# A two-layer mixer block and its follow-up on one core: input projection on raw input, weight splits on VectorE, feed-forward parts made tile by tile

## Chip, cores and metric

The kernel runs on one core of a Trainium2 chip. The metric is the device time of one execution in microseconds (us); smaller is better. Before the change three runs took 2217.0, 2222.6 and 2223.59 us, median 2222.6.

## The reference, cut to what matters

512 tokens of width 1024 pass two layers (`DEPTH = 2`), and then a second, different block that the change doesn't touch. One layer is:

```python
h = rmsnorm(x, attn_norm[l])
z = h @ w_in[l]                                    # 1024 -> 2256 columns
(c_q, c_kv, k_rope, g_q, g_k, g_v, g_lr, g_g, r_q, r_k, r_v, r_g) = jnp.split(z, ...)
y_a = mla_branch(...)     # q = rmsnorm(c_q) @ w_uq, k and v = rmsnorm(c_kv) @ w_ukv, causal softmax, 4 heads
y_b = gla_branch(...)     # gated linear attention, 4 heads, its gate from g_lr
y_c = retention_branch(...)                        # 4 heads, rope on q and k
x = x + jnp.concatenate([y_a, y_b, y_c], -1) @ w_out[l]
h = rmsnorm(x, ffn_norm[l])
u = h @ ffn_w_up[l]                                # 1024 -> 2 * 2816
a, bv = u[..., :D_FF], u[..., D_FF:]
x = x + (silu(causal_dwconv(a)) * bv) @ ffn_w_down[l]
```

`rmsnorm` multiplies by a gain for each feature and by one factor for each token (the inverse root of the mean square). The factor is the same for all features of a token, so it may be applied after the product with the weights: that is what the kernel calls raw.

## The kernel before, in words

**Layout.** `x_t` holds x turned: features on the 128 partitions, 8 tiles of 512 tokens. Every product with a weight is made three times in the float32r format: activations and weights are each split into a high part (a rounded copy, `h_hi`, `w_hi`) and a low part (value minus high part, `h_lo`, `w_lo`), and high x high, high x low and low x high are summed. Lines L823 to L825 issue them in `product`.

**Weights** come in chunks of up to 1024 x 256 (1 MB) into two slots of `w_raw`, alternately. Chunk c goes through: a DMA on SyncE's queue (`load`, issued when the low half of chunk c-2 has been made), `w_hi` copied by ScalarE (`high`, `next_high`, when TensorE is done with chunk c-2), `w_lo` subtracted by GpSimd (L1010, in the first part of a layer) or by VectorE (`split_low`, L1835, in the feed-forward), and two tiles of products on TensorE, each 128 output features x 512 tokens, or 2 x 128 tokens x 256 columns for those whose output is wanted with tokens on the partitions. A counter `w_split` releases TensorE. All of it is written out by hand, each engine with its own list of instructions in order, and semaphores between them.

**Order of a layer** (chunks and tiles by number: chunk c has tiles 2c and 2c+1):
- Chunk 0 is multiplied with raw parts of x (made at the end of the layer before, without the token factor), `raw_tiles`. Meanwhile the token factor `rms_a` is formed, and VectorE and ScalarE form normed parts h_hi and h_lo (`parts_dve`, L812 and L797; `parts_act`, L786) in place, one of the 8 feature tiles after the other. Chunk 1 (`two_tiles`, L847 to L849) follows these step by step, with the small matmul of the linear attention's gate (`gate_low`, L1122) in its middle.
- Chunks 2 to 8 (tiles 4 to 17) use the normed parts. ScalarE copies each finished tile out of PSUM (L1418). Between the tiles stand the matmuls of the linear attention: for seven decay levels VectorE forms two products (L1939, L1941) and a difference (L1880), ScalarE an exponential, TensorE 32 small matmuls (`pairs`, L1087), and VectorE keeps a part of their results with a predicated copy (`keep`, L1890). Turn, state update and output of this branch follow (L1094, L1101, L1111, L1114).
- Chunks 9 to 15 are the up-projections of q, k and v, with contraction over 3 and 2 tiles only, and in between the matmuls that swap halves for the rope (L1165 to L1168). VectorE applies the rope (`rope`, L1823 to L1827). Its table comes by a DMA ahead of the load of chunk 15, after all of q's tiles.
- The attention goes over 16 instances (`att_pe`, `att_act`, `att_dve`): scores (L466), mask and maximum (L557, L562), exponential (L521), turn (L475), copy (L515), values (L486), and after every fourth the normalisation (L543, L547). The retention branch runs in its gaps, as functions in `fill` by instance number: rope halves, pairs, weights, turn, update, output.
- The out-projection (chunks 16 to 19) needs y turned, a tile at a time (`turn_y`, L1210), and its parts (`high_y` L1563, `low_y` L1994). Two tiles are turned in the attention, six in the first chunk. Before these, `lin_gated` (L1931) must be done for the retention, and GpSimd scales `y_mla` by the factor of each head (L1026).
- ScalarE copies each output tile, VectorE adds it to x_t (L2016), squares and sums it (L1789, L1791). After the last tile the statistic is formed (L763), and then parts of x for the feed-forward (L1592, L1994), again raw.
- Up loop: 22 chunks of 11 pairs; down loop: 12 chunks. Then the next layer.

## Time and profile before

| | |
|---|---|
| median of 3 runs | 2222.6 us |
| the profiled execution's own time | 2222.46 us |
| its span | 2220.5 us |
| mean granted TensorE clock | 0.967 |
| TensorE busy | 2054.5 us, 93% |
| VectorE busy | 1121.5 us, 51% |
| ScalarE busy | 855.1 us, 39% |
| GpSimd busy | 435.7 us, 20% |

Both layers run the same loop body. Layer 0's ends at about 700 us, layer 1's at about 1358 us, and the second block takes the rest. Busy TensorE isn't TensorE at full speed: matmuls overlap, and their length grows when the granted clock is at its lower level (0.50, 1.2 GHz) and not the upper one (1.00, 2.4 GHz).

### The profile page before, as it was taken

How to read it: one execution, taken by the hardware profiler on the slowest of the kernel's cores; microseconds unless marked ns; L12 is line 12 of the kernel's file. 1: busy time of each engine (PE TensorE's matmuls, PEld its weight loads, DVE VectorE, ACT ScalarE, POOL GpSimd, SP SyncE). 2: the span in 40 equal slices, each digit the busy share in tenths (PEclk: the TensorE clock that was granted, in tenths of full speed). 3: DMA queues.
4: the chain of work that ended last, by engine and by line, in shares of the span. 5: the costliest groups of instructions: out<-in, count | busy, mean ns of one | idle time of the engine just before them, and what ended most of it. 6: DMA issues, size and time to landing. Idle time of an engine off the chain costs nothing.

```text
span 2220.5 us, 28741 instructions
## 1 busy us (share of the span) xinstructions
PE 2054.5 (93%) x10802; PEld 1647.7 (74%) x10802; DVE 1121.5 (51%) x1222; ACT 855.1 (39%) x1212; POOL 435.7 (20%) x178
## 2 busy tenths in 40 slices
PE   5998889999999998889999998899999899899987
PEld 3786578888886886678888886887777566788765
DVE  6754665555536755665555446515552522313353
ACT  4444443333213444333333223234445455534333
POOL 3323030000000313030000001432222222343441
PEclk9998989999999999999999999999999899999998
DMA  5213023333232213023333223323322112132230
GB/s 139 76 41 114 1 70 82 94 94 94 85 104 74 76 42 114 1 76 92 97 95 94 85 90 119 115 67 102 80 85 66 52 48 77 57 105 84 69 104 38
DMA packets 236697, 177.72 MB, mean 80 GB/s; under 512 B 11700, under 2 KB 231215, under 8 KB 236207
## 3 DMA queue, kind: packets, MB, share of 16 engines
q1 hardware_dynamic: 235664, 174.74, 26.3%
q8 instruction: 69, 1.13, 0.2%
q10 hardware_dynamic: 575, 1.50, 0.2%
q0 software_dynamic: 352, 0.05, 0.1%
q14 instruction: 37, 0.30, 0.0%
HBM read 167.87 MB, written 2.10 MB: 77 GB/s over the span
## 4 chain that ended last, share of the span: by engine, by line
PE 68%; DVE 11%; issue 10%; POOL 5%; ACT 4%; DMA 2%; SPq 1%; ACTq 0%; DVEq 0%; POOLq 0%
PE ps L823 19%; PE ps L825 19%; PE ps L824 18%; POOL w_lo L1010 4%; PE ps L466 2%; PE ps L591 2%; PE ps L604 1%; PE ps L615 1%; POOL w_lo L1036 1%; ACT w_hi L1654 1%; PE ps L486 1%; PE ps L475 1%; DVE h_lo L2197 1%; DVE qk L2092 1%; DMA gains_in<-in_ffn_conv_w_dram 0%
## 5 line engine op out<-in xcount | busy, mean ns | idle before, releaser
L823 PE MATMUL ps<-h_hi,w_hi 128*128 128x512 f32 x1488 | 599.1, 403 | 17.6 <-ACT qk L1418 6.2
L825 PE MATMUL ps<-h_hi,w_lo 128*128 128x512 f32 x1488 | 587.1, 395 | 0.0
L824 PE MATMUL ps<-h_lo,w_hi 128*128 128x512 f32 x1488 | 582.9, 392 | 0.0
L1036 POOL TENSOR_TENSOR w_lo<-w_raw,w_hi 128x1024 fp32r<-128x1024 f32 (+1 forms) x118 | 264.9, 2268 | 930.2 <-ACT w_hi L1654 930.2
L823 PEld LDWEIGHTS ps<-h_hi,w_hi 128*128 128x128 f32 x1488 | 282.6, 190 | 83.7 <-DVE h_lo L1994 9.0
L825 PEld LDWEIGHTS ps<-h_hi,w_lo 128*128 128x128 f32 x1488 | 281.6, 189 | 65.1
L824 PEld LDWEIGHTS ps<-h_lo,w_hi 128*128 128x128 f32 x1488 | 282.3, 190 | 60.6 <-issue 1.0
L1010 POOL TENSOR_TENSOR w_lo<-w_raw,w_hi 128x2048 fp32r<-128x2048 f32 (+2 forms) x42 | 154.3, 3676 | 702.3 <-ACT w_hi L1425 684.7
L1425 ACT ACTIVATE w_hi<-w_raw 128x2048 fp32r<-128x2048 f32 (+3 forms) x108 | 186.7, 1729 | 203.1 <-PE ps L825 196.2
L1835 DVE TENSOR_TENSOR w_lo<-w_raw,w_hi 128x2048 fp32r<-128x2048 f32 (+1 forms) x68 | 151.6, 2230 | 195.3 <-ACT w_hi L1425 193.2
L823 PE MATMUL ps<-w_hi,h_hi 128*128 128x256 f32 x480 | 139.0, 290 | 6.9 <-POOL w_lo L1036 6.4
L823 PE MATMUL ps<-hid_hi,w_hi 128*128 128x512 f32 x352 | 138.7, 394 | 0.0
L825 PE MATMUL ps<-hid_hi,w_lo 128*128 128x512 f32 x352 | 138.0, 392 | 0.0
L824 PE MATMUL ps<-hid_lo,w_hi 128*128 128x512 f32 x352 | 136.6, 388 | 0.0
L824 PE MATMUL ps<-w_lo,h_hi 128*128 128x256 f32 x480 | 136.0, 283 | 0.0
L825 PE MATMUL ps<-w_hi,h_lo 128*128 128x256 f32 x480 | 135.7, 283 | 0.0
L1654 ACT ACTIVATE w_hi<-w_raw 128x1024 fp32r<-128x1024 f32 (+1 forms) x118 | 108.2, 964 | 13.9 <-DMA w_raw<-in_w_in_dram 12.1
L1603 ACT ACTIVATE rms_a<-a_pad,g 128x512 f32<-128x512 f32 x44 | 35.9, 816 | 173.5 <-DVE a_pad L2031 173.5
L823 PEld LDWEIGHTS ps<-w_hi,h_hi 128*128 128x128 f32 x480 | 92.4, 193 | 9.4 <-POOL w_lo L1036 6.6
L2036 DVE SCALAR_TENSOR_TENSOR rms_a<-a_pad,g,rms_a 128x512 f32<-128x512 f32 x88 | 66.2, 752 | 57.1 <-ACT rms_a L1603 50.5
L699 DVE TENSOR_TENSOR ps<-ps,win 128x768 f32<-128x768 f32 x32 | 30.9, 966 | 124.9 <-PE ps L591 124.4
L824 PEld LDWEIGHTS ps<-w_lo,h_hi 128*128 128x128 f32 x480 | 92.8, 193 | 0.7 <-issue 0.5
(367 smaller groups left out, 3009.0 us busy)
## 6 DMA issues: line engine op xcount, KB each, us to landing
w_raw<-in_ffn_w_up_dram SPq DMA_DIRECT2D x88, 512.0 KB, 4.8
w_raw<-in_w_in_dram SPq DMA_DIRECT2D x41, 1024.0 KB, 5.1
w_raw<-in_w_in_dram SPq DMA_DIRECT2D x32, 512.0 KB, 4.9
w_raw<-in_ffn_w_down_dram SPq DMA_DIRECT2D x32, 512.0 KB, 4.3
w_raw<-in_w_out_dram SPq DMA_DIRECT2D x12, 1024.0 KB, 4.8
w_raw<-in_ffn_w_down_dram SPq DMA_DIRECT2D x16, 384.0 KB, 3.3
swapped<-qk SPq DMA_DIRECT2D x96, 64.0 KB, 2.0
w_raw<-in_w_mem_kv_dram SPq DMA_DIRECT2D x4, 1024.0 KB, 4.8
```

Of the source, the lines that this page charges most:

```text
L466: ins = pe.matmul(score_ps(banks, i, c0, n), lhs, rhs, start=a, stop=b)
L591: ins = pe.matmul(ps[:, b, c:c + n], lhs, rhs, start=True, stop=True)
L823: pe.matmul(dst, lh, rh, start=first and j == 0, stop=False)
L824: pe.matmul(dst, lh, rl, start=False, stop=False)
L825: ins = pe.matmul(dst, ll, rh, start=False, stop=last and j == len(order) - 1)
L1010: pool.tensor_tensor(w_lo[:, slot, 0:n], w_raw[:, slot, 0:n], w_hi[:, slot, 0:n].bitcast(F32), ALU.subtract).then_inc(sem("w_split"), 1)
L1036: ins = pool.tensor_tensor(w_lo[:, slot, q * n:q * n + n], w_raw[:, slot, q * n:q * n + n], w_hi[:, slot, q * n:q * n + n].bitcast(F32), A ...
L1425: act.activation(w_hi[:, slot, 0:n], w_raw[:, slot, 0:n], ACT.Copy).then_inc(sem("w_high"), 1)
L1603: act.activation(conv[:], a_pad[:, s, 2:S + 2], ACT.Identity, scale=g[:, bass.ds(G_CONVW + 2 * KF + f, 1)], bias=g[:, bass.ds(G_CONVB + f, ...
L1654: act.activation(w_hi[:, slot, q * n:q * n + n], w_raw[:, slot, q * n:q * n + n], ACT.Copy).then_inc(sem("w_high"), 1)
L1835: dve.tensor_tensor(w_lo[:, slot, 0:n], w_raw[:, slot, 0:n], w_hi[:, slot, 0:n].bitcast(F32), ALU.subtract).then_inc(sem("w_split"), 1)
L2036: dve.scalar_tensor_tensor(conv[:], a_pad[:, s, w:w + S], g[:, bass.ds(G_CONVW + w * KF + f, 1)], conv[:], ALU.mult, ALU.add).then_inc(sem ...
```

## The change

It does the following in both layers:
- The whole input projection (chunks 0 to 8) uses the raw parts. No normed parts are formed. VectorE takes the feature tiles out of PSUM itself (`evict`) and multiplies by `rms_a`; for token tiles ScalarE applies the factor as a scale for each partition, in two half copies (`copy_tokens`), after TensorE has turned `rms_a` into columns (`tok_rms`).
- All low halves of the layers' weights after the first two are made by VectorE (`split`), at written places of its list; GpSimd does nothing in the layers after those two.
- The decay levels start one tile earlier. The chunk of the retention's gate comes before the one of its values, and the rope part of w_uq before the two others. The rope's table is loaded after chunk 4. The retention's swap matmuls and ropes come ahead of the attention and not in it.
- The out-projection's parts have buffers of their own (`y_hi`, `y_lo`), its tiles the banks 0, 2, 1, 3. `y_mla` is scaled by VectorE in four parts within the attention and behind it. Four tiles of y are turned in the attention, four in the first chunk of the out-projection.
- VectorE adds each output tile to x_t right from PSUM, and the feed-forward's parts of this tile follow at once, in `h_hi` and `h_lo`. The first up tile stands before the statistic, and the up loop is rotated by one tile.
- Tanh for both gates is done in one place; two changes of ScalarE's function table go in each layer.

```diff
@@ SyncE
-                    if c == C_OUT - 1:
-                        sp.wait_ge(sem("tile_done"), upto(sp, "tile_done", 2 * C_UKV))
+                    if c == 4:
                         sp.dma_start(tab[:], A["c_rope"]).then_inc(sem("tab_loaded"), tick("tab_loaded", 16))
@@ GpSimd
-            with pool.Fori(0, DEPTH) as l:
...
-                    split(c, c % 2, SPLIT_K[c])
...
-                        pool.tensor_tensor(ym, ym, stats[:, 96:112].unsqueeze(2).to_broadcast([P, 16, VDIM]),
-                                           ALU.mult).then_inc(sem("ymla"), tick("ymla"))
@@ TensorE
-                        two_tiles(pe, 1, KD, h_hi, h_lo, (2, 3), (P, P), PART["x"], before={4: (0,)}, turn=gate_low)
-                    elif t > 3:
+                        features(pe, 1, 0, KD, h_hi, h_lo, 2, last=False, order=range(4))
+                        gate_low()
+                        features(pe, 1, 0, KD, h_hi, h_lo, 2, first=False, order=range(4, KD)).then_inc(sem("tile_done"), tick("tile_done"))
+                    elif t > 2:
                         tile(t, KD, h_hi, h_lo, kind)
...
-                    if 6 <= t < 6 + len(LEVELS):
+                    if 5 <= t < 5 + len(LEVELS):
...
+                    if t == 2 * C_UKV + 1:
+                        pe.wait_ge(sem("roped"), upto(pe, "roped", 1))
+                        for j in range(2):
+                            pe.matmul(ps[:, 4 + 3 * j, :], swap32, lin[:, 2 + j, :], start=True, stop=True).then_inc(sem("rot"), tick("rot"))
...
+                att_pe(pe, mla_groups(), prob, prob_t, fill={
+                    0: partial(ret_pairs, 0), 2: partial(ret_pairs, 2), 4: ret_turn, 6: ret_update, 8: partial(ret_out, 0),
+                    9: partial(ret_out, 1), 12: partial(turn_y, 0), 13: partial(turn_y, 1), 14: partial(turn_y, 2),
+                    15: partial(turn_y, 3)})
...
+                two_tiles(pe, C_OUT % 2, KD, y_hi, y_lo, OUT_BANKS[0:2], (P, P), PART["y"], Y_ORDER,
+                          before={3: (4, 5), 4: (6,), 5: (7,)}, turn=turn_y)
...
+                up_tile(0, 0, 0)
                 sum_stat(pe, 8)
-                with pe.Fori(0, KF // 2) as i:
+                with pe.Fori(0, KF // 2 - 1) as i:
+                    up_tile(i, 0, 1)
+                    up_tile(i, 1, 0)
+                    up_tile(i, 1, 1)
+                    up_tile(i + 1, 0, 0)
@@ VectorE
-                parts_dve(dve, 0, normed(dve, xs, col(G_ATTN, 8), rms_a[:], 0), hi, lo, fulls1, after={3: raw_scaled})
+                diff(0)
+                evict(2, lin[:, 0], LIN_DK ** -0.5)
+                evict(3, lin[:, 1])
+                level(0)
+                split(3)
+                evict(4, cq[:, 0])
+                keep(0, len(LEVELS))
...
+                for i in range(len(LEVELS)):
+                    if i < 3:
+                        evict(5 + i, cq[:, 1 + i])
+                    keep(i + 1, i)
+                    if i + 1 < len(LEVELS):
+                        level(i + 1)
+                    if i % 2 == 0:
+                        split(4 + i // 2)
+                evict(12, lin[:, 2])
...
+                split(14)
+                rope(3, lin[:, 2], ps[:, 4, :], tab[:, 2], tab[:, 3], lin[:, 2], tmp[:, 2])
+                split(15)
+                rope(4, lin[:, 3], ps[:, 7, :], tab[:, 2], tab[:, 3], lin[:, 3], tmp[:, 2])
...
+                    0: partial(ret_weights, 0), 1: ret_decayed, 2: partial(ret_weights, 2), 3: partial(split, 16),
+                    4: partial(mla_squares, 0), 5: partial(split, 17), 6: partial(lin_update, 1, um_r, (3, 7), lambda t: ret_c),
+                    7: partial(mla_scaled, 0), 8: partial(mla_squares, 1), 10: partial(lin_squares, 1, o_sb_r, um_r),
+                    11: partial(mla_scaled, 1), 12: lambda: (mla_squares(2), lin_gated(1, o_sb_r, sig_r, LIN["ret"]["gate"])),
+                    13: partial(low_y, 0), 14: lambda: (mla_squares(3), low_y(1))})
+                mla_scaled(2)
+                low_y(2)
+                low_y(3)
+                mla_scaled(3)
...
+                    dve.tensor_tensor(x_t[:, m], x_t[:, m], ps[:, OUT_BANKS[m], :], ALU.add).then_inc(sem("tile_copied"), 1)
...
+                    if m % 2:
+                        split(C_OUT + 2 + m // 2)
```

## Rows read from the trace of the kernel before

**Rows 1.** The page, the chain that ended last: shares of the span by engine.
```profile
PE 68%; DVE 11%; issue 10%; POOL 5%; ACT 4%; DMA 2%; SPq 1%; ACTq 0%; DVEq 0%; POOLq 0%
```

**Rows 2.** Busy time by windows, layer 1; columns as in the first line.
```profile
core 0: us, PE busy (x) PEld busy (x) DVE busy (x) ACT busy (x) POOL busy (x), PEclk, DMA share, GB/s
706.60:726.40 19.80, 14.87 (x51) 9.99 (x51) 17.66 (x19) 6.54 (x9) 4.68 (x1) 0.91 0.17 55
726.40:835.90 109.50, 103.53 (x845) 91.48 (x844) 63.92 (x56) 46.30 (x62) 30.05 (x7) 0.95 0.17 50
835.90:870.20 34.30, 28.30 (x137) 21.65 (x135) 16.09 (x15) 20.06 (x30) 15.18 (x8) 1.00 0.38 123
870.20:925.40 55.20, 52.37 (x278) 34.36 (x278) 35.20 (x65) 22.59 (x57) 4.21 (x1) 0.94 0.12 39
925.40:980.20 54.80, 49.50 (x217) 40.29 (x216) 32.79 (x32) 15.50 (x21) 17.92 (x4) 0.94 0.18 50
980.20:988.20 8.00, 2.23 (x4) 0.52 (x3) 6.57 (x4) 7.49 (x10) 4.52 (x1) 0.68 0.22 55
988.20:1358.70 370.50, 370.50 (x1608) 303.86 (x1609) 200.11 (x216) 116.79 (x114) 0.00 (x0) 0.99 0.32 94
```

**Rows 3.** The same view, three windows of layer 0.
```profile
66.50:173.30 106.80, 100.28 (x844) 88.84 (x843) 64.55 (x56) 46.14 (x61) 30.02 (x7) 0.98 0.17 52
173.30:212.30 39.00, 28.32 (x136) 21.64 (x135) 20.36 (x15) 20.44 (x30) 19.12 (x8) 0.91 0.41 135
267.90:321.80 53.90, 48.66 (x216) 39.68 (x216) 32.79 (x32) 15.40 (x21) 17.92 (x4) 0.97 0.18 50
```

**Rows 4.** TensorE's waits, 700 to 1000 us: total us, times, longest us.
```profile
PE ps L1087 <- DVE gl L1941: 6.0, 3, 2.2
PE ps L847 <- DVE h_lo L797: 4.9, 3, 3.0
PE ps L466 <- DVE qr L1827: 4.8, 1, 4.8
PE ps L1210 <- DVE tm L1931: 4.1, 1, 4.1
PE ps L823 <- DVE h_lo L1994: 2.9, 1, 2.9
...
PE ps L475 <- ACT prob_t L515: 2.0, 2, 1.4
```

**Rows 5.** Busy time by windows again, three short stretches of layer 1.
```profile
720.80:723.60 2.80, 2.71 (x6) 2.15 (x7) 2.35 (x5) 0.63 (x1) 0.00 (x0) 0.50 0.71 224
760.30:768.70 8.40, 8.34 (x83) 7.99 (x84) 5.22 (x7) 3.12 (x5) 0.00 (x0) 0.80 0.39 126
768.60:775.30 6.70, 6.70 (x82) 6.50 (x80) 5.34 (x3) 2.51 (x2) 3.81 (x1) 1.00 0.00 0
```

**Rows 6.** Timeline of all engines, 754.4 to 760.4 us: start, length, instruction.
```profile
754.43 4.60 POOL L1010 TENSOR_TENSOR w_lo<-w_raw,w_hi 128x2048 fp32r<-128x2048 f32 x1 [8.20 <-ACT w_hi L1425]
...
754.94 4.64 DVE L1939 TENSOR_TENSOR gl<-lin,gl 128x512 f32<-128x512 f32 x1
```

**Rows 7.** The page, costliest groups: count, busy us, mean ns, idle before.
```profile
L1425 ACT ACTIVATE w_hi<-w_raw 128x2048 fp32r<-128x2048 f32 (+3 forms) x108 | 186.7, 1729 | 203.1 <-PE ps L825 196.2
L1835 DVE TENSOR_TENSOR w_lo<-w_raw,w_hi 128x2048 fp32r<-128x2048 f32 (+1 forms) x68 | 151.6, 2230 | 195.3 <-ACT w_hi L1425 193.2
```

**Rows 8.** VectorE's groups by shape, 726 to 836 us, columns as above.
```profile
L1890 DVE COPY_PREDICATED amat<-levels,ps 128x2048 f32<-128x2048 uint8 x8 | 19.9, 2488 | 17.3 <-issue 15.5 <-DVE gl L1880 1.8
L1939 DVE TENSOR_TENSOR gl<-lin,gl 128x512 f32<-128x512 f32 x7 | 17.1, 2446 | 0.2
L1880 DVE TENSOR_TENSOR gl<-gl 128x512 f32<-128x512 f32 x7 | 4.8, 692 | 0.2
```

**Rows 9.** TensorE's timeline, one row of the attention, one behind it.
```profile
874.50 3.29 PE L1174 MATMUL ps<-lin,cm 128*128 128x512 f32 x4
...
940.81 0.60 PE L1210 MATMUL ps<-cm,y_mla 128*128 128x128 f32 x4
```

More of the change, by code:

```diff
@@ L1155, in _ @@
                 for t in range(2 * C_UQ, 2 * C_UKV):
[L1156 to L1166 removed]
+                    tile(t, 3, cq_hi[:, 0:3], cq_lo[:, 0:3])
@@ L1169, in _ @@
                 pe.wait_ge(sem("tile_copied"), upto(pe, "tile_copied", 2 * C_OUT))
-                pe.wait_ge(sem("roped"), upto(pe, "roped", 3))
-                def ret_halves():
-                    for j in range(2):
-                        pe.matmul(ps[:, 3 * j, :], swap32, lin[:, 2 + j, :], start=True, stop=True).then_inc(sem("rot"), tick("rot"))
+                pe.wait_ge(sem("roped"), upto(pe, "roped", 5))
                 def ret_pairs(first):
-                    if first == 0:
-                        pe.wait_ge(sem("roped"), upto(pe, "roped", 5))
-                    else:
+                    if first:
@@ new lines, in up_tile @@
+                def up_tile(i, s, half):
+                    c = C_UP + 2 * i + s
+                    if half == 0:
+                        split_ready(c)
+                    pe.wait_ge(sem("tile_copied"), upto(pe, "tile_copied", 2 * c + half - 3))
+                    features(pe, s, half, KD, h_hi, h_lo, 2 * s + half,
+                             ready=PART["ffn"] if s + half == 0 else None).then_inc(sem("tile_done"), 1)
+                up_tile(0, 0, 0)
+                sum_stat(pe, 8)
@@ L1933, in lin_gated, with level @@
                     dve.wait_ge(sem("y_lin"), upto(dve, "y_lin"))
-                diff(0)
-                keep(0, len(LEVELS))
-                for i in range(len(LEVELS)):
+                def level(i):
                     dve.wait_ge(sem("lvl_exp"), upto(dve, "lvl_exp", i + 1))
```

358 lines of the change are left out of this document (191 added, 167 removed).

## The prediction

> **What bounds the kernel now.** I read the page first: the chain that ended last is 68% TensorE and 11% VectorE [rows 1], so time is set by TensorE's queue wherever something else is late. Next came the windows by stage, layer 1 and layer 0 [rows 2, 3]. The reader is to see two kinds of stretch. In the feed-forward loops (988.2 to 1358.7) TensorE is busy for 370.5 of 370.5 us with 1608 matmuls, 0.230 us each: nothing can be won there. In the other windows of layer 1 the busy time falls short: 4.9 us in the second weight chunk, 6.0 in the rest of the input projection, 6.0 in the up-projections of the attention, 2.8 in the attention, 5.3 in the out-projection and 5.8 before the feed-forward loop. That is 31 us in one layer, and the clock column is below 1.00 in most of these windows, so part of the busy time is stretched as well. The change works on just these windows; up loop, down loop and second block keep their instructions (one up tile moves, one chain starts earlier).
>
> Third, the waits [rows 4]. All that matter name VectorE: 6.0 us in 3 waits for the decay levels (L1941), 4.8 us for the last rope (L1827), 4.1 us for the gated retention output (L1931), 4.9 us in 3 waits for the low parts of h (L797), 2.9 us for those of the feed-forward (L1994). Fourth, why VectorE is late [rows 6]: GpSimd splits a weight chunk from 754.43 for 4.60 us; VectorE's product of two SBUF tiles, issued at 754.94, takes 4.64 us and ends when GpSimd does. The group of that line has 7 instructions with a mean of 2446 ns, against 692 ns for the same shape in the next group [rows 8]. VectorE is held for the whole of GpSimd's instruction.
>
> The Trainium skill, "SBUF — State Buffer", section "Who interferes with whom", says the same: a VectorE instruction with two SBUF inputs contends with a GpSimd instruction that reads SBUF, and whoever issues first keeps the shared ports for its whole instruction. By that rule all two-input VectorE work beside a split is exposed, and with GpSimd silent none is; the trace agrees, with 4.64 against 0.69 us [rows 6, 8].
>
> Fifth, the price of a wait beyond itself [rows 5]: after the 2.2 us wait, pairs and a token tile took 8.4 us at a mean clock of 0.80; the same work without a wait in front took 6.7 us at 1.00. So each such wait costs another 1.7 us at the lower level. Six matmuls behind the 3.0 us wait for L797 [rows 4] took 2.8 us at 0.50, against 6 x 0.230 = 1.4: 1.4 us lost.
>
> **Change part by part**, layer 1 unless said.
>
> A. Chunk 1 no longer waits for normed parts. Now: 19.8 us [rows 2]. After: the raw h parts of chunk 0 are used again, and chunk 1's low half has long been made. 48 x 0.230 = 11.0, the gate matmul 1.0 (an estimate: 4 to 5 plain matmuls), four one-column turns 0.4: 12.4. Gain 7.4. The gate waits for VectorE's two evictions (2 x 0.7 us behind the raw tiles), while TensorE has 12 matmuls, 2.8 us, in front of it: covered. The 16 instructions of the normed parts (8 products, 8 subtractions) leave VectorE and 8 copies leave ScalarE; 10 evictions, of 0.69 us like other 512-wide products [rows 8], come to VectorE instead, token tiles get two half copies on ScalarE. I take the same gain in layer 0.
>
> B. Chunks 2 to 8. Now 109.5 us in layer 1, 106.8 in layer 0. The 3 waits (6.0) and their lower clock (3 x 1.7) go, leaving 98.4 in either: gains 11.1 and 8.4. That holds only if VectorE keeps up. Per pair of tiles it has two times (predicated copy 2.49 + q 0.69 + k 0.69 + difference 0.69 + eviction 0.69) = 10.5 and one split of 2.3 (mean 2230 ns over two sizes, most of them the larger [rows 7]): 12.8, with some 0.04 between instructions 13.3. TensorE takes 2 x 6.7 = 13.4. Equal, so the order decides. After the pairs of a tile end, the copy, q and k take 4.0 us, and TensorE wants them 5.6 us later; difference, split and eviction (3.8) lie behind, pushing the next copy by about 1.1 us. Slack at the worst place is near 0.5 us. The token tiles (four of eight) have no eviction on VectorE. I take no wait. The weight side: next high half is copied once the slot's last tile is done, about 1.9 us (mean 1729 ns over four sizes [rows 7]), then 2.3 us of split, while 13.4 us of the other slot run: covered. Waiting behind split(8) there are the evictions and q and kv parts, some 8 us, against 27 us until it is needed.
>
> C. Up-projections. Now 34.3 us (39.0 in layer 0), of which 6.0 us is unbusy; in layer 0, 10.7. The table loads with chunk 4 and not at the end, and the ropes meet no GpSimd split. Content 28.3; the two swap matmuls of the retention come in, 1.9 us (an estimate: half of the 3.3 us they have now at the lower clock, rounded up [rows 9]); at the end one ScalarE copy behind a 1.9 us high half, 1.3. Together 31.5: gains 2.8 and 7.5. These chunks are short, 2.8 us for two tiles of the smallest, and a tile copy of some 0.7, a high half and a split of a quarter of the width, some 0.6 each by the share of rows 7, and the gaps make 2.2, with a rope of 2.2 in VectorE's queue in front. The split of chunk 15 comes only 0.8 us ahead. Without that cover each of four chunks would pay up to 2.2.
>
> D. Attention. Now 55.2. The swap matmuls go (-3.3 [rows 9]), the waits for prob_t too (-2.0 [rows 4]), and after 1.3 us of idle instead of 4.8 the first scores run faster: the clock of 0.94 means 12% of the window at half speed, 3.3 us lost; I take back 1.5. In come two turns of y at most 0.6 each [rows 9] (+1.2), and VectorE's fills. Two splits (4.6), two scalings, two gatings (2.5) now sit between the maxima; three ropes and a silu go. Following the queue, the fifth value product waits for the first normalisation (+1.4), the last score for squares, gating and third normalisation (+1.7). Gain 2.5. Bounds: all of it hidden, 5.6; each split fully on the path, -2.1.
>
> E. Out-projection. Now 54.8 and 53.9 us. Contents 192 x 0.230 = 44.2, four turns left 2.4. After the last value product VectorE does normalisation 1.0, squares 1.4, low part 0.8 before the second k step may start, 3.3 us, while TensorE has 1.4: wait 1.9, then 0.2 for the turns; the low clock again, 1.4. Sum 50.1: gains 4.7 and 3.8. GpSimd's 4 us scaling of y_mla becomes four small VectorE ones of 0.7.
>
> F. Feed-forward start. Now 8.0, and six matmuls at half speed behind it (1.4). After: the parts of x follow tile by tile. VectorE needs per tile addition, square, low part and sum, 4 x 0.73 = 2.9, and per two tiles a split 2.3: 8.1 of the 11.0 us that TensorE needs. The last part is ready 3.5 us after the last tile (high half 1.9 on ScalarE first, copy, low part); the first up tile wants it after 7 steps, 4.8 us. Only the statistic remains, 0.5. Gain 8.9. rms_f then comes some 2 us behind the first up tile; four banks hide this.
>
> Sum, layer 1: 7.4 + 11.1 + 2.8 + 2.5 + 4.7 + 8.9 = 37.4; layer 0: 7.4 + 8.4 + 7.5 + 2.5 + 3.8 + 8.9 = 38.5. Together 75.9; for short waits where I found slack below 1 us (B, C) I give back 1 per layer. 2220.5 - 73.9 = 2146.6 for the span. The profiled execution took 2222.46, 2.0 more than its span, and the median of the runs is 2222.6. Forecast 2148.6, said as 2148.
>
> **Rivals.**
> 1. VectorE becomes the bound in B. For: 13.3 against 13.4. Against: only three of eight tiles carry an eviction. If four levels are 0.6 late, each with 1.7 of lower clock: 9 us a layer, 2166. Chance 0.15.
> 2. The fills stall the softmax. For: a split is one instruction of 2.3 us that a maximum can't pass. Each split and the gating on the path: 2 x 2.3 + 2.5 = 7 a layer, 2162. Chance 0.12.
> 3. The waits of E and D don't appear, since the chains overlap better than I follow them: -(1.9 + 1.4 + 1.4 + 1.7) a layer, 2135. Chance 0.13.
> 4. Slower. Weight loads are issued only after the low half of the chunk two before; that now stands in VectorE's queue. The 36 splits of both layers would each have to be late by 76/36 = 2.1 us beyond their slack to eat the gain, 2.3 for a loss over 0.3%: 2231. Against: in the up loop, VectorE already makes its splits, and TensorE is busy throughout [rows 2]. Chance 0.02.
> 5. The change doesn't do what it says: TensorE merely waits elsewhere, for ScalarE, within 0.3%: 2220. ScalarE is busy 46.3 of 109.5 us [rows 2], so I give 0.01.
> The forecast has 0.57.
>
> **Numbers.** 0.3% (some 7 us) is about what this measurement can tell from no change. Range 2134 to 2168: it takes in rivals 1 to 3 and the bounds of D, and leaves out some 1 in 10. Faster 0.97, same 0.01, slower 0.02.
>
> **What the profile after would show.** GpSimd silent between the first two splits and the second block; L1939's product at 0.69; no wait of the level pairs; stages near 12.4, 98, 31, 53, 50 and 0.5 us; the feed-forward loops at 370. Wrong: level pairs waiting for the predicated copy (rival 1), first value products waiting for normalisation by more than 2 us (rival 2), or TensorE waiting for w_lo from VectorE anywhere (rival 4).

## The result, and the profile after

| | before | after |
|---|---|---|
| median of the runs | 2219.8 us (4 runs, 2209.2 to 2223.6) | 2161.4 us (4 runs, 2154.1 to 2167.2) |
| ratio, 95% interval | | 0.9743, 0.9691 to 0.9794 |
| profiled execution, its span | 2222.46, 2220.5 us | 2166.44, 2164.7 us |
| VectorE, GpSimd busy | 1121.5, 435.7 us | 1105.0, 283.8 us |

The kernel is 2.6% faster. The forecast was 2148, the range 2134 to 2168. The span fell by 55.8 us (26.7 in layer 1, 27.0 up to its start, 2.1 in the second block) where the prediction's sum had 73.9.

Busy time by windows of the changed kernel, layer 1; the stages are those of [rows 2], and the feed-forward's start is now its first up tile, 936.10 to 942.00:

```profile
core 0: us, PE busy (x) PEld busy (x) DVE busy (x) ACT busy (x) POOL busy (x), PEclk, DMA share, GB/s
679.60:693.10 13.50, 13.50 (x62) 10.61 (x61) 9.23 (x10) 7.21 (x10) 0.00 (x0) 1.00 0.46 159
693.10:792.20 99.10, 99.10 (x846) 87.60 (x844) 71.41 (x72) 42.09 (x58) 0.00 (x0) 1.00 0.19 56
792.20:823.00 30.80, 28.92 (x139) 22.34 (x138) 14.61 (x21) 15.24 (x23) 0.00 (x0) 1.00 0.32 103
823.00:887.50 64.50, 61.97 (x281) 42.02 (x282) 37.52 (x63) 25.16 (x64) 0.00 (x0) 0.76 0.10 33
887.50:936.10 48.60, 46.60 (x212) 37.60 (x211) 34.58 (x43) 13.86 (x17) 0.00 (x0) 1.00 0.22 60
936.10:942.00 5.90, 5.90 (x27) 4.67 (x26) 4.24 (x5) 2.53 (x2) 0.00 (x0) 1.00 0.16 42
942.00:1305.00 363.00, 363.00 (x1587) 297.64 (x1586) 195.76 (x210) 116.16 (x113) 0.00 (x0) 1.00 0.33 96
```

The same view, layer 0: the up-projections and the attention.

```profile
160.70:191.70 31.00, 28.95 (x140) 22.37 (x139) 14.61 (x21) 15.24 (x23) 0.00 (x0) 1.00 0.33 102
191.70:256.10 64.40, 61.89 (x282) 41.94 (x283) 37.51 (x63) 25.18 (x64) 0.00 (x0) 0.76 0.10 33
```

The reader is to see one row that doesn't fit. Every other stage of layer 1 runs at a clock of 1.00 and takes what was forecast to within 1.5 us. The attention became longer, 64.5 us against 55.2 in [rows 2], though less stands still in it: TensorE is busy for 62.0 us of it, and its clock is 0.76 where it was 0.94.

TensorE's waits in the changed kernel, 680 to 942 us (total us, times, longest us):

```profile
PE ps L848 <- DVE y_lo L2051: 2.0, 1, 2.0
PE ps L476 <- ACT prob_t L516: 1.9, 1, 1.9
PE ps L467 <- ACT v_mla L1428: 1.9, 1, 1.9
PE ps L1201 <- DVE tm L1959: 0.6, 1, 0.6
```

All waits of [rows 4] for the level pairs, the low parts of h, the rope and the feed-forward's parts are gone. The 11.8 us that the attention is above the forecast (64.5 against 52.7) are not in waits: TensorE stands still for 2.5 us of it. Windows again, inside the attention of layer 1:

```profile
825.00:831.00 6.00, 6.00 (x30) 4.47 (x28) 3.42 (x9) 2.52 (x11) 0.00 (x0) 0.51 0.00 0
...
843.00:849.00 6.00, 6.00 (x15) 2.99 (x15) 5.00 (x7) 1.63 (x6) 0.00 (x0) 0.50 0.43 146
849.00:853.00 4.00, 4.00 (x15) 3.46 (x14) 0.65 (x2) 1.56 (x5) 0.00 (x0) 0.57 0.79 262
853.00:859.00 6.00, 6.00 (x32) 3.78 (x31) 4.80 (x10) 1.55 (x4) 0.00 (x0) 1.00 0.01 1
```

TensorE is busy 6.00 of 6.00 us at its lower level (0.50, 1.2 GHz) for some 27 us on end, in both layers. In the kernel before, the attention started at the lower level too:

```profile
212.30:222.00 9.70, 9.68 (x23) 5.84 (x24) 4.70 (x11) 1.65 (x7) 0.00 (x0) 0.50 0.33 108
870.20:877.30 7.10, 7.10 (x17) 4.28 (x18) 2.58 (x8) 2.00 (x8) 4.21 (x1) 0.52 0.68 222
877.30:884.40 7.10, 6.63 (x41) 4.18 (x41) 6.37 (x12) 1.44 (x6) 0.00 (x0) 1.00 0.22 73
```

There the clock rose 9.7 us (layer 0) and 7.1 us (layer 1) into it: 1.4 us behind the two retention swaps of 512 columns in layer 0, in the last half microsecond of them in layer 1 [rows 9]. The change had moved just these two out of the attention, into the up-projections, where they run at the upper level. TensorE's groups by shape, 792 to 823 us (the trace has two records for each of the two matmuls):

```profile
L1165 PE MATMUL ps<-lin,cm 128*128 128x512 f32 x4 | 1.9, 592 | 0.0
```

That gives a theory (the clock theory: without the swaps the attention's first part is only short matmuls, and the clock stays low through them) and a rival: VectorE's new fills, two weight splits above all, hold the softmax up, and the clock merely follows.

### The profile page after: what moved, and what is told of

Read it like the earlier page. It is cut to its first block, busy times and chain, and to the rows that moved or that the text cites. A ratio compares the mean times of both kernels' runs of the same rounds, so it can differ in the third digit from the quotient of the medians.

```text
span 2164.7 us, 28562 instructions
## 1 busy us (share of the span) xinstructions
PE 2050.3 (95%) x10818; PEld 1649.5 (76%) x10818; DVE 1105.0 (51%) x1254; ACT 827.6 (38%) x1186; POOL 283.8 (13%) x136
## 4 chain that ended last, share of the span: by engine, by line
PE 84%; DVE 7%; ACT 4%; DMA 2%; POOL 1%; issue 1%; SPq 0%; ACTq 0%; DVEq 0%
PE ps L824 23%; PE ps L826 22%; PE ps L825 22%; PE ps L467 3%; PE ps L592 2%; PE ps L605 1%; PE ps L616 1%; POOL w_lo L1024 1%; PE ps L487 1%; PE ps L1075 1%; ACT w_hi L1667 1%; PE ps L476 1%; PE ps L1102 1%; DMA w_raw<-in_w_out_dram 1%; PE ps L757 1%
## 5 line engine op out<-in xcount | busy, mean ns | idle before, releaser
L824 PE MATMUL ps<-h_hi,w_hi 128*128 128x512 f32 x1408 | 565.8, 402 | 11.8 <-ACT qk L1428 6.2
L826 PE MATMUL ps<-h_hi,w_lo 128*128 128x512 f32 x1408 | 553.5, 393 | 0.0
L825 PE MATMUL ps<-h_lo,w_hi 128*128 128x512 f32 x1408 | 549.8, 390 | 0.0
L1848 DVE TENSOR_TENSOR w_lo<-w_raw,w_hi 128x2048 fp32r<-128x2048 f32 (+3 forms) x108 | 222.6, 2061 | 234.7 <-ACT w_hi L1435 229.1
L824 PEld LDWEIGHTS ps<-h_hi,w_hi 128*128 128x128 f32 x1408 | 266.0, 189 | 73.3 <-issue 9.6
L826 PEld LDWEIGHTS ps<-h_hi,w_lo 128*128 128x128 f32 x1408 | 265.0, 188 | 61.1
L825 PEld LDWEIGHTS ps<-h_lo,w_hi 128*128 128x128 f32 x1408 | 265.8, 189 | 57.0 <-issue 1.4
L824 PE MATMUL ps<-w_hi,h_hi 128*128 128x256 f32 x448 | 127.1, 284 | 4.4 <-POOL w_lo L1024 4.4
L825 PE MATMUL ps<-w_lo,h_hi 128*128 128x256 f32 x448 | 125.5, 280 | 0.0
L826 PEld LDWEIGHTS ps<-w_hi,h_lo 128*128 128x128 f32 x448 | 85.5, 191 | 0.0
```

Of the source, the lines that this page charges most:

```text
L824: pe.matmul(dst, lh, rh, start=first and j == 0, stop=False)
L825: pe.matmul(dst, lh, rl, start=False, stop=False)
L826: ins = pe.matmul(dst, ll, rh, start=False, stop=last and j == len(order) - 1)
L1848: dve.tensor_tensor(w_lo[:, slot, 0:n], w_raw[:, slot, 0:n], w_hi[:, slot, 0:n].bitcast(F32), ALU.subtract).then_inc(sem("w_split"), 1)
```

## The experiments

All are edits of the changed kernel. Attention is the time from the first score matmul to the out-projection's first product in the profiled execution, layer 0 and layer 1, with the mean clock. Spans and stages are those of one execution each; the medians are of four to six.

| kernel | median us | ratio to before, 95% | span | attention, clock |
|---|---|---|---|---|
| changed | 2161.4 | 0.9743 (0.9691 to 0.9794) | 2164.7 | 64.4 at 0.76, 64.5 at 0.76 |
| e1_burst | 2149.2 | 0.9669 (0.9646 to 0.9692) | 2147.9 | 56.8 at 0.94, 55.4 at 0.97 |
| e2_fill | 2142.1 | 0.9638 (0.9615 to 0.9661) | 2140.3 | 58.7 at 0.85, 53.6 at 0.97 |
| e3_both | 2140.4 | 0.9643 (0.9619 to 0.9666) | 2138.3 | 53.8 at 1.00, 55.0 at 0.98 |
| e4_pool | 2180.5 | 0.9826 (0.9797 to 0.9855) | 2175.2 | 59.9 at 0.83, 59.8 at 0.83 |
| e5_stat_first | 2168.6 | 0.9761 (0.9735 to 0.9786) | 2160.6 | 62.9 at 0.78, 58.4 at 0.85 |
| e6_low_first | 2144.0 | 0.9655 (0.9632 to 0.9679) | 2137.7 | 57.0 at 0.94, 53.8 at 1.00 |
| e7_pool_two | 2137.9 | 0.9630 (0.9602 to 0.9657) | 2136.1 | 54.0 at 0.97, 54.0 at 0.97 |
| e8_one_each | 2149.7 | 0.9680 (0.9644 to 0.9715) | 2144.6 | 60.9 at 0.83, 53.3 at 1.00 |
| e9_parts_late | 2172.4 | 0.9782 (0.9748 to 0.9815) | 2173.8 | 62.8 at 0.78, 64.4 at 0.76 |
| e10_swaps_back | 2150.7 | 0.9692 (0.9660 to 0.9724) | 2144.0 | 59.7 at 0.94, 59.8 at 0.91 |
| e11_both_more | 2140.5 | 0.9652 (0.9621 to 0.9683) | 2136.9 | 54.4 at 0.97, 53.5 at 1.00 |
| e12_back_fill | 2148.8 | 0.9682 (0.9650 to 0.9714) | 2150.8 | 61.3 at 0.86, 58.9 at 0.97 |

A span is a rough measure of an edit: the second block, which no edit touches, differs by itself. Here is everything behind layer 1 in the changed kernel and in e10_swaps_back, 9.0 us apart; in e1_burst it took 859.9 us, in e2_fill, e7_pool_two and e8_one_each 853.4.

```profile
1305.00:2164.70 859.70, 785.55 (x4427) 625.96 (x4425) 342.16 (x369) 364.74 (x588) 265.80 (x118) 0.96 0.26 79
```

```profile
1293.30:2144.00 850.70, 783.80 (x4432) 625.37 (x4431) 341.67 (x370) 365.50 (x589) 266.02 (x118) 0.97 0.26 79
```

The firmer measure is the length of the stage that an edit touches.

### Long matmuls at the attention's start

e1_burst adds work behind the first scores, e2_fill in the wait ahead of them, e3_both at both places.

```diff
+                pe.wait_ge(sem("roped"), upto(pe, "roped", 3))               # e2, e3
+                for _ in range(2):
+                    pe.matmul(ps[:, 5, :], swap64, qr[:, 0, :], start=True, stop=True)
                 pe.wait_ge(sem("tile_copied"), upto(pe, "tile_copied", 2 * C_OUT))
...
+                def burst():                                                 # e1, e3
+                    for _ in range(2):
+                        pe.matmul(ps[:, 7, :], swap32, lin[:, 2, :], start=True, stop=True)
...
-                    0: partial(ret_pairs, 0), 2: partial(ret_pairs, 2), 4: ret_turn,
+                    0: lambda: (burst(), ret_pairs(0)), 2: partial(ret_pairs, 2), 4: ret_turn,
```

> The changed kernel, with two 512-column fp32 matmuls added on TensorE in each layer, behind the first score group of the attention, ahead of the retention pairs; their result is not used. They stand where the kernel before had its two retention swaps. Clock theory: the 12 us that each layer's attention took above the forecast are TensorE's low granted clock (0.50 for some 27 us), and it is low for long because the retention swaps, behind which the clock rose in the kernel before, are no longer in the attention. Then the clock rises some 10 us into the attention, the attention takes 55 to 58 us in place of 64.5 (the added work of about 3 us included), and the span falls from 2164.7 to between 2147 and 2155. Rival: the two weight splits that VectorE now makes inside the attention (and the other added fills) hold the softmax up, and the clock is only a consequence of TensorE's waits; then the attention keeps its 64.5 us plus up to 3.3 us of added work, and the span is 2165 to 2172.

> The changed kernel, with two 512-column fp32 matmuls added in each layer just before TensorE waits for the last copy of the up-projections (the 1.9 us wait ahead of the first scores); their result is not used. Clock theory, first form: the fall to 0.50 at the start of the attention is set off by that idle time; filled, the clock stays at 1.00 and the attention takes about 53 us in place of 64.5, span about 2142. Clock theory, second form: what sets the clock off is the attention's own thin start (many short matmuls with their loads), and the idle time before it only hastens it; then less than 2 us per layer change, span 2161 to 2168. Rival (VectorE's fills hold the softmax up): no change, span 2164 to 2168.

> Both additions: two unused 512-column matmuls ahead of the attention's first wait, and two behind its first score group, in each layer. Clock theory: the attention takes 53 to 57 us, at or below the shorter of the two kernels with one addition each; span 2142 to 2152. If the first addition alone keeps the clock up, this one is slower than it by the 1.7 us per layer of the second pair at full clock. Rival (VectorE's fills): 64.5 us plus the added work, span 2168 to 2172.

The attention by windows, layer 0 and layer 1: first e1_burst, then e2_fill, then e3_both.

```profile
191.56:248.38 56.82, 53.18 (x287) 35.54 (x287) 37.32 (x63) 25.27 (x64) 0.00 (x0) 0.94 0.12 38
815.22:870.60 55.38, 51.52 (x286) 34.85 (x287) 37.34 (x63) 25.20 (x64) 0.00 (x0) 0.97 0.11 39
```

```profile
190.16:248.86 58.70, 55.99 (x282) 37.68 (x283) 37.41 (x63) 25.24 (x64) 0.00 (x0) 0.85 0.11 37
815.87:869.43 53.56, 49.91 (x283) 34.36 (x283) 37.32 (x63) 25.25 (x64) 0.00 (x0) 0.97 0.13 40
```

```profile
189.70:243.47 53.77, 50.12 (x286) 33.34 (x287) 37.32 (x63) 25.25 (x64) 0.00 (x0) 1.00 0.12 40
811.37:866.36 54.99, 51.27 (x286) 34.59 (x287) 37.33 (x63) 25.25 (x64) 0.00 (x0) 0.98 0.12 39
```

More work made the kernel faster, by 12 to 21 us at the median. The cleanest pair is layer 1 of the changed kernel and of e2_fill: inside the attention they have the same instructions (282 or 283 records of TensorE, 63 of VectorE, 64 of ScalarE) and take 64.5 us at 0.76 and 53.6 us at 0.97. VectorE's busy time is 37.5 and 37.3. So 10.9 us are the clock's, and the rival, which had no change or a loss in all three, falls. Two results differ from what was expected: e3_both's span of 2138.3 lies below its range, and e2_fill did in layer 1 what the first form of the theory said and in layer 0 half of it.

The form of the theory that blames the wait alone falls too. In e2_fill the wait ahead of the scores is down to 0.24 us in layer 0, and the clock still fell 3 us later, for some 17 us; in e1_burst it was 1.00 from the first score of layer 1 on, behind a wait of 1.8 us, and fell only at the attention's end (0.63 from 866.00 to 870.60). What the added matmuls change is how often and how long it is low, not by a fixed amount.

The Trainium skill, "TensorE: Matmul & The Clock Gate", section "What's actually happening", has the lower clock as the default and activity as what releases it, and its section "HAM oscillation — how this bites in real kernels" blames waits for the fall. That more work brings the clock up agrees with e1_burst (0.94 and 0.97 in place of 0.76). That an engine without idle time stays at 0.50 for 27 us is not what the page lets one expect: here it was 6.00 busy of 6.00 us.

### The step itself undone

e10_swaps_back adds no work: the two swaps go back behind the first score group, VectorE's retention rotation with them, and the retention's later steps follow two groups later. e12_back_fill is the same with the matmuls of e2_fill.

```diff
-                    if t == 2 * C_UKV + 1:
-                        pe.wait_ge(sem("roped"), upto(pe, "roped", 1))
-                        for j in range(2):
-                            pe.matmul(ps[:, 4 + 3 * j, :], swap32, lin[:, 2 + j, :], start=True, stop=True).then_inc(sem("rot"), tick("rot"))
...
-                    0: partial(ret_pairs, 0), 2: partial(ret_pairs, 2), 4: ret_turn, 6: ret_update, 8: partial(ret_out, 0),
-                    9: partial(ret_out, 1), 12: partial(turn_y, 0), 13: partial(turn_y, 1), 14: partial(turn_y, 2),
+                    0: ret_halves, 2: partial(ret_pairs, 0), 4: partial(ret_pairs, 2), 6: ret_turn, 8: ret_update,
+                    10: partial(ret_out, 0), 11: partial(ret_out, 1), 12: partial(turn_y, 0), 13: partial(turn_y, 1), 14: partial(turn_y, 2),
...
-                rope(3, lin[:, 2], ps[:, 4, :], tab[:, 2], tab[:, 3], lin[:, 2], tmp[:, 2])
...
+                    0: ret_rope, 1: ret_decayed, 2: partial(ret_weights, 0), 3: partial(split, 16),
```

> The changed kernel with one step undone and no work added: the two retention swap matmuls (512 columns each) are moved back from the fourth up-projection tile into the attention, behind its first score group, and VectorE makes the retention rotation there, as in the kernel before; the retention's later steps follow two groups later. Clock theory: it is this move that left TensorE at the low granted clock; with the swaps back in the attention the clock rises some 5 to 10 us into it, the attention takes 55 to 60 us in place of 64.5 (about 1.5 us of swaps and 1 us of short waits included), the up-projection stage loses 1 us, and the span is 2146 to 2158. Rival (only added work keeps the clock up, the place of the swaps is without effect, or the later retention steps hold up the last groups): attention 63 us or more, span 2162 or more.

> The same kernel with the swaps back in the attention, and with the two unused 512-column matmuls in the wait ahead of the first scores, as in e2_fill. Clock theory: full clock from the start in most layers, attention 53 to 56 us, span 2135 to 2145, as with the two additions of e3_both but with one useful pair in the place of one unused. Rival: the late retention steps cost more than the clock gives back: 2145 to 2160.

Windows of e10_swaps_back: around the swaps in layer 0, the same in layer 1, and a third place of layer 1.

```profile
189.54:196.54 7.00, 7.00 (x17) 4.21 (x18) 2.46 (x7) 3.45 (x8) 0.00 (x0) 0.53 0.00 1
196.54:202.54 6.00, 5.65 (x36) 3.47 (x34) 5.49 (x10) 1.01 (x4) 0.00 (x0) 0.98 0.00 0
816.06:822.06 6.00, 6.00 (x18) 3.46 (x19) 2.57 (x8) 3.45 (x8) 0.00 (x0) 0.72 0.00 0
822.06:828.06 6.00, 5.28 (x36) 3.40 (x35) 5.52 (x10) 1.01 (x4) 0.00 (x0) 1.00 0.00 0
834.40:841.40 7.00, 6.98 (x21) 3.81 (x21) 6.46 (x10) 2.99 (x9) 0.00 (x0) 0.55 0.46 152
```

The next score follows the swap matmuls at 822.05, and from there the clock is 1.00: the low stretch of 27 us has become one of some 3 us here (0.72 over 6.0 us) and 7 us in layer 0 (0.53 over 7.0 us). The median falls by 10.7 us with nothing added, and all six runs (2141.4 to 2152.7) lie below all four of the changed kernel (2154.1 to 2167.2), though the intervals of the ratios overlap a little; the span of 2144.0 is 2 us below the range expected. Of the 20.7 us by which the span fell, 9.5 are in the two attentions and 9.0 in the second block.

e10_swaps_back moves the later retention steps too, so by itself it doesn't single out the swaps. e1_burst does: it adds two such matmuls at that place and changes nothing else. The table's clocks say the same. In the eight attentions that have no long matmul at their start (changed, e4_pool, e5_stat_first, e9_parts_late) the mean clock is 0.76 to 0.85. In the fourteen that have at least two behind the first scores (e1, e3, e6, e7, e10, e11, e12) it is 0.86 to 1.00. The two others lie across both: e2_fill, whose pair stands ahead of the scores (0.85 and 0.97), and e8_one_each (0.83 and 1.00). So the move of the swaps is shown as what left the clock low for so long.

The step back isn't free: the attention is 59.7 us at 0.94 and 59.8 at 0.91, only 4.7 us shorter than in the changed kernel, since my order of the later fills brings new waits. Its waits, layer 1:

```profile
PE ps L467 <- ACT v_mla L1430: 2.7, 1, 2.7
PE ps L476 <- ACT prob_t L516: 2.3, 2, 1.9
PE ps L848 <- DVE y_lo L2055: 2.0, 1, 2.0
PE ps L487 <- DVE y_mla L548: 1.4, 1, 1.4
PE ps L1075 <- DVE lin L1842: 0.7, 1, 0.7
```

The clock falls once more at about 835, behind the wait of 1.4 us for y_mla, and stays low for some 6 us. e12_back_fill missed what the clock theory promised: in layer 1 it has the clock at 0.97, and its attention still takes 58.9 us; in layer 0 the clock was 1.00 through the swaps, fell 6 us behind them, at 200.5, and stayed low for some 17 us. Long matmuls at the start don't hold the clock for the whole attention. The rival of that pair (the late retention steps cost more than the clock gives back) held.

### VectorE's two splits in the attention

e7_pool_two is e3_both with the splits of chunks 16 and 17 on GpSimd.

```diff
                 def split(c):
-                    split_low(c, c % 2, SPLIT_K[c])
+                    if c not in (16, 17):
+                        split_low(c, c % 2, SPLIT_K[c])
...
+                for c in (16, 17):                  # in GpSimd's program, per layer
+                    pool.wait_ge(sem("w_split"), upto(pool, "w_split", c))
+                    split(c, c % 2, SPLIT_K[c])
```

> The kernel with both additions (e3_both: attention at full clock throughout, 53.8 and 55.0 us), with only the two weight splits that fall inside the attention (chunks 16 and 17 of a layer) put back on GpSimd; all other splits stay on VectorE. Clock theory: with the clock up, the attention's length is TensorE's own work, so the 4.6 us of VectorE time that goes away change nothing: attention 53 to 55.5 us, span 2136 to 2142. Rival (VectorE's fills hold the softmax up, the clock apart): the attention loses up to 4.6 us per layer, span 2129 to 2133. A third possibility: GpSimd's two products slow VectorE's work beside them, as they did in the kernel before, and the attention grows by 1 us or more per layer.

Its attention by windows, layer 0 and layer 1:

```profile
190.28:244.26 53.98, 51.40 (x286) 34.94 (x287) 32.94 (x61) 25.25 (x64) 7.88 (x2) 0.97 0.12 40
811.26:865.25 53.99, 51.39 (x287) 34.93 (x287) 32.93 (x61) 25.25 (x64) 7.89 (x2) 0.97 0.12 40
```

VectorE has 4.4 us less to do, and the attention keeps its 54 us (e3_both: 53.8 and 55.0). The two splits are nearly off the path, but not wholly. One wait of TensorE is in the attention of e3_both, in both layers, and not in e7_pool_two:

```profile
PE ps L487 <- DVE y_mla L548: 1.1, 1, 1.1
```

These 1.1 us a layer are what the two splits hold up once the clock is high, against the 4.6 of the rival; e7_pool_two gives about as much back at the attention's end, where its clock falls (0.83 over the last 10 us). In the changed kernel, with TensorE at the lower level, this wait isn't there, and it is mostly VectorE that waits for TensorE's scores in the attention of layer 1:

```profile
DVE ps L558 <- PE ps L467: 11.9, 8, 4.8
```

One fill is on the path in all of them, near the attention's end: squares and gating keep VectorE from 876.82 to 880.76, the last maximum stands behind them, and TensorE waits 1.9 us for prob_t. The forecast had this (1.7 us).

### The dose

e8_one_each has one added matmul at each place in place of two; e11_both_more is e7_pool_two with three behind the first scores.

> The kernel with both additions, at half the dose: one unused 512-column matmul at each of the two places in place of two. If that is enough to keep TensorE at full clock through the attention, it saves the half of the added work: 53 to 54 us per attention, span 2134 to 2140. If the dose matters, the clock falls in one of the layers or in both and the attention takes 57 to 65 us there: span 2143 to 2165.

> The kernel with both additions and two splits on GpSimd (e7_pool_two, whose profiled span was 2136.1 and whose runs lay between 2135 and 2147), with three unused matmuls in place of two behind the first score group. If a larger dose makes full clock certain in every run, the median falls from 2137.9 to about 2136 and the spread of the runs narrows, in spite of 0.9 us more work per layer; if the clock was lost elsewhere, the median is 2138 to 2141.

One matmul at each place is not enough to be sure: the six runs of e8_one_each lie between 2136.2 us at a mean clock of 0.983 and 2162.1 us at 0.969. That is one program with one input, and the clock accounts for about the whole spread: a low stretch costs half its length, so the estimate is 0.014 of 2150 us, 30 us, and 26 were measured. Two at each place don't settle it in every execution either: the runs of e3_both lie between 2136.0 and 2148.6 us. Three in place of two brought nothing (2140.5 against 2137.9, intervals overlap); the theory's 2136 wasn't reached. Nor were the runs closer together (2134.7 to 2144.1).

### All splits back on GpSimd

```diff
                 def split(c):
-                    split_low(c, c % 2, SPLIT_K[c])
+                    pass
...
+            with pool.Fori(0, DEPTH) as l:
+                layer[pool] = l
+                for c in range(2, C_UP + 2):
+                    if c == 2:
+                        pool.wait_ge(sem("w_split"), upto(pool, "w_split", 2))
+                    split(c, c % 2, SPLIT_K[c])
```

> The changed kernel with one part undone: the low halves of the weights of all chunks of a layer from the third on are split off on GpSimd again, as in the kernel before; all else stays. By the prediction's terms the input projection goes from 99.1 us back towards 109.5 and 106.8 us, the later up-projections towards 34.3 and 39.0 us in place of 30.8, and the out-projection towards 54 us in place of 48.6; the attention loses two splits on VectorE but its element-wise work slows beside GpSimd again. Theory (the split's move carries more than half of the gain): span 2180 to 2200. Rival 1 (the rest of the reordering carries the gain, and the splits are hidden on either engine): span 2160 to 2170. Rival 2 (VectorE's splits hold up the softmax): the attention falls from 64.5 to some 55 us per layer, whatever the other stages do.

The input projection from the gate on, layer 1, by windows: the changed kernel, then e4_pool, and e4_pool's waits there.

```profile
683.70:794.10 110.40, 110.40 (x888) 95.41 (x887) 77.21 (x79) 49.07 (x70) 0.00 (x0) 1.00 0.23 69
```

```profile
692.10:811.70 119.60, 113.70 (x888) 98.36 (x888) 80.94 (x71) 49.03 (x70) 32.73 (x8) 0.97 0.21 64
```

```profile
PE ps L1081 <- DVE gl L1973: 5.9, 3, 2.7
```

VectorE's groups by shape in that stretch: the decay product in e4_pool, and in the changed kernel.

```profile
L1971 DVE TENSOR_TENSOR gl<-lin,gl 128x512 f32<-128x512 f32 x7 | 15.7, 2245 | 0.2
```

```profile
L1965 DVE TENSOR_TENSOR gl<-lin,gl 128x512 f32<-128x512 f32 x7 | 4.8, 693 | 0.2
```

The three waits for the levels come back (5.9 us, 6.0 in [rows 4]) with their lower clock (0.03 of 119.6 us, 3.6): 9.2 us in this stage, 9.1 in layer 0. The product takes 2245 ns on average beside GpSimd, 693 without it. The up-projections lose another 1. The attention was 4.6 us shorter, its low stretch some 5 us of full-speed time less costly, which is again the clock and not the splits: TensorE stands still for 2.5 us of it in either kernel. The out-projection is unchanged at 48.5 us: its gain is not the splits'. The feed-forward's start is not unchanged. There TensorE waits in both layers, where the changed kernel shows no wait, and VectorE's last low part takes 4.56 us beside GpSimd's split (0.75 for the one before):

```profile
PE ps L824 <- DVE h_lo L2082: 2.5, 1, 2.5
```

```profile
953.05 4.56 DVE L2082 SCALAR_TENSOR_TENSOR h_lo<-x_t,g,h_hi 128x512 fp32r<-128x512 f32 x1 [0.84 <-ACT h_hi L1611]
```

A window from the first product of layer 0's out-projection to the first score of layer 1 leaves the attention and its clock out. It has 566.90 us in the changed kernel and 582.02 in e4_pool: 15.1 us, of which 9.2 are the input projection, about 1.3 the up-projections, and the other 4.6 this wait and the lower clock behind it.

```profile
256.11:823.01 566.90, 563.02 (x2887) 463.98 (x2885) 332.91 (x364) 198.38 (x225) 0.00 (x0) 1.00 0.30 87
```

```profile
259.85:841.87 582.02, 568.78 (x2888) 467.75 (x2886) 339.00 (x346) 198.29 (x224) 63.15 (x19) 0.99 0.29 85
```

The expectation missed all the same: the span of 2175.2 lies below the 2180 to 2200 of its theory, and the 19.1 us that the median loses are a third of the change's gain, not more than half.

### The feed-forward's start

e9_parts_late makes the parts behind the last out-projection tile; e5_stat_first puts the statistic ahead of the first up tile.

```diff
                         next_high(t // 2)                       # e9, ScalarE
-                    act.wait_ge(sem("tile_copied"), upto(act, "tile_copied", t + 1))
+                act.wait_ge(sem("tile_copied"), upto(act, "tile_copied", 2 * C_OUT + KD))
+                for m in range(KD):
                     act.activation(h_hi[:, m], x_t[:, m], ACT.Copy, scale=col(G_FFN + m, 1)).then_inc(sem("h_hi"), tick("h_hi"))
...
-                up_tile(0, 0, 0)                                # e5, TensorE
                 sum_stat(pe, 8)
-                with pe.Fori(0, KF // 2 - 1) as i:
+                with pe.Fori(0, KF // 2) as i:
```

> The changed kernel (no added matmuls) with the feed-forward's parts made only when all eight out-projection tiles are added to the residual, on ScalarE and on VectorE alike, as in the kernel before; the first up tile still stands ahead of the statistic. The prediction's step F had this: TensorE's idle time at the feed-forward's start fell from 8.0 to 0.5 us per layer. Theory: 4 to 8 us of idle come back per layer, span 2172 to 2181 at the same clock. Rival (the parts are hidden by the first up tile, which takes them one by one): under 2 us per layer, span 2165 to 2168.

> The changed kernel (no added matmuls), with the feed-forward's start in the old order: the sum of the squares first, then the up tiles in one loop of two chunks, not rotated. By the prediction the first up tile ahead of the statistic was worth about 1.4 us of TensorE's idle time per layer, of the 8.9 us for the whole step: span 2166 to 2169 against 2164.7. Rival (the rotated loop costs as much in its branch as it saves): 2163 to 2165.

TensorE's waits behind 890 us: e9_parts_late, then e5_stat_first.

```profile
PE ps L824 <- DVE h_lo L2084: 5.3, 1, 5.3
```

```profile
PE ps L764 <- DVE rms_a L2076: 4.3, 1, 4.3
```

Late parts cost 5.3 us of waiting in either layer; the median rises by 11.0. Without the rotated loop TensorE waits 4.3 us for the statistic, for which the changed kernel shows no wait, and the median rises by 7.2. Both medians are within reach of chance, since the intervals of the ratios overlap with that of the changed kernel. The window between the attentions, as above, is the firmer measure: first e9_parts_late, then e5_stat_first.

```profile
253.65:828.73 575.08, 565.56 (x2886) 465.46 (x2885) 333.11 (x364) 198.76 (x224) 0.00 (x0) 0.99 0.29 86
```

```profile
253.67:827.81 574.14, 565.66 (x2887) 465.38 (x2886) 332.88 (x364) 198.19 (x224) 0.00 (x0) 0.99 0.29 86
```

Against 566.90 us this is 8.2 and 7.2 us a layer, more than the waits, since the clock is lower behind them. The expectation of e5_stat_first had 1.4 for its part; its rival (nothing) falls. The span of e5_stat_first was lower than expected, since the attention of its layer 1 happened to be 6 us shorter at 0.85, with no long matmul added.

### One wait more

e6_low_first is e3_both with `14: lambda: (low_y(1), mla_squares(3))`, the low part first.

> The kernel with both additions, and VectorE makes the second low part of the attention's output before the squares of the last head group in its last fill but one. Aim: the 2.0 us for which the out-projection waits for VectorE's low part, a wait that the prediction had at 1.9 us. If it is the order of VectorE's fills, the wait falls to 1 us or less, 1 to 1.5 us per layer, span 2135 to 2137. If the wait only moves to the last head group's factor, no change, span 2138 to 2141.

It missed. The wait for y_lo stays at 1.9 us, now in two pieces. The wait for y_mla below is no effect of this edit; e3_both has the same one.

```profile
PE ps L848 <- DVE y_lo L2058: 1.9, 2, 1.4
...
PE ps L487 <- DVE y_mla L548: 1.1, 1, 1.1
```

## Why the prediction was right, and where it was wrong

The direction and the range held, with the median 13 us above the forecast, and the mechanism held in every stage but the attention. That the time stayed in the range is in part luck: the attention alone missed by 23 us over both layers, and its own bounds did not reach that far. Layer 1, saved time by its steps:

| step | predicted | measured |
|---|---|---|
| A, second weight chunk | 7.4 | 19.8 - 13.5 = 6.3 |
| B, rest of the input projection | 11.1 | 109.5 - 99.1 = 10.4 |
| C, up-projections | 2.8 | 34.3 - 30.8 = 3.5 |
| D, attention | 2.5 | 55.2 - 64.5 = -9.3 |
| E, out-projection | 4.7 | 54.8 - 48.6 = 6.2 |
| F, feed-forward's start and loop | 8.9 | 378.5 - 368.9 = 9.6 |
| allowance | -1.0 | 0 |
| sum | 36.4 | 26.7 |

**A, B, C** were right to within 1.1 us. B rests on GpSimd's silence: e4_pool gives 9 us of it back. One reading under it was loose: VectorE's product in [rows 6] does not end when GpSimd's split does (759.03) but at 759.58, 0.55 us later, which fits a product that is held and then takes little less than its own 0.69 us. Rival 1 (VectorE the bound) didn't come; VectorE is busy for 71.4 of 99.1 us, so the count of 13.3 against 13.4 us a pair of tiles was too tight.

**D** is the step that failed: "after 1.3 us of idle instead of 4.8 the first scores run faster ... I take back 1.5". The clock gave back nothing. By its mean, 15.5 us (0.24 of 64.5) are lost to it where it had been 3.3; 10.9 of them show in the time, against e2_fill's layer 1, which has waits of its own. Nor did the idle time before the scores fall to 1.3 us: it was 2.1 and 1.9. I tied the lower clock to the wait ahead of it and left out what ends it. The row was there, the swaps of [rows 9] at the attention's start, and I counted them only as 3.3 us that go away. The bounds of D (5.6 to -2.1) didn't reach -9.3 either. The rest of the step was right: at a clock near 1.00 the same instructions take 53.6 us (e2_fill, layer 1), against 52.7 forecast, with 1.1 us of waiting for the first normalisation (forecast 1.4) and 1.9 for the last score (1.7). Rival 2 had nearly the right time, 2162, for the wrong reason: its two splits and the gating were to cost 7.1 us a layer, but the splits cost 1.1 at the upper clock and nothing at the lower one, and the wait behind the gating was in the forecast already.

**E** was right in its wait (2.0 us, forecast 1.9) and 1.5 us too dear: the stage shows a clock of 1.00, and the 1.4 us for a lower one weren't paid. Rival 3 came true in that part and, in the changed kernel, in the 1.4 us for the first normalisation; its two other waits came.

**F** was right: 8.9 forecast, 9.6 measured, and 8.2 and 7.2 us a layer come back when either half is undone (e9_parts_late, e5_stat_first). A part of it rests on GpSimd's silence as well, which the prediction didn't say: e4_pool loses about 4.6 us here.

**Rivals 4 and 5** didn't come: TensorE waits nowhere for a w_lo that VectorE makes.

Layer 0's attention went from 55.6 us (212.3 to 267.9) to 64.4. So over both layers D fell short by 11.3 + 11.8 = 23.1 us; the other steps, the allowance and 2.1 us in the second block (less than that block differs by itself) give 5.0 back: 73.9 - 18.1 = 55.8.

What stays open is what makes the clock fall at the attention's start in one execution and not in another, and how long it then stays low: with the same instructions 27 us in the changed kernel and some 17 us in layer 1 of e5_stat_first. The fastest version is the changed kernel with long matmuls at that start, and it gives 2138 to 2140 us (e7_pool_two, e3_both, whose intervals overlap), 1% below the changed kernel, though four 512-column matmuls per layer do nothing in it.

## What to carry to other kernels

Before a long matmul is moved out of a stretch of short ones, look in the clock column at what ends the lower clock there: here two matmuls, 1.9 us together, were moved, and the attention behind them ran some 11 us a layer longer than it does at the upper clock; even unused ones in their place paid for themselves. A stage in which TensorE is busy throughout can still be at half speed; compare its length at the same instruction count, not its busy share. Taking the weight splits off GpSimd was worth 15 us a layer, but only where two-input work of VectorE lay on TensorE's path: 9.2 in the input projection, 4.6 at the feed-forward's start, some 1.3 in the up-projections, nothing in the out-projection. And when a new fill is judged by the wait that it brings, the clock must be high: 1.1 us of waiting were hidden while TensorE was slow.

## What the runs showed of the hardware

TensorE stayed at 0.50 for 27 us while it was busy 6.00 of 6.00 us, with matmuls of 128 to 384 columns and their weight loads between them. Two matmuls of 512 columns behind the first scores ended or averted this in both layers of e1_burst and e10_swaps_back. They didn't prevent a later fall (e12_back_fill, layer 0: 6 us behind them, for some 17 us). Whether it falls at the attention's start differs between two layers of one execution (e2_fill: 0.85 and 0.97) and between executions (e8_one_each: 26 us between runs). And a 512-wide product of VectorE with both operands in SBUF took 693 ns alone and up to 4.64 us beside GpSimd [rows 6], on average 2245 ns in e4_pool; a 512-wide low part took 4.56 us beside GpSimd and 0.75 without it (e4_pool).
